# Squares of the query heads: turned by TensorE and summed by ScalarE, in place of two-column fp32 matmuls

## The chip, the cores and the metric

The kernel runs on one core of a Trainium2 chip. The metric is device time in microseconds of one execution. Four compute engines work side by side, each with its own instruction queue: TensorE (PE in the profile, its weight loads PEld), VectorE (DVE), ScalarE (ACT) and GpSimdE (POOL). SyncE (SP) issues most of the transfers. They wait for each other on semaphores only.

## The reference

Seven residual steps are computed on 512 tokens of width 1024: a feed-forward network, a mixer of three parts (windowed attention, a convolution, attention over a memory), another feed-forward network, and then two blocks of which the first has sparse attention and the second a short convolution as its mixer, each with a feed-forward network of its own. What matters here is the normalization of each head of 64 features of the queries, in both attention mixers:

```python
def rms_norm(x, g):
    y = xf * lax.rsqrt(jnp.mean(xf * xf, axis=-1, keepdims=True) + EPS)
    return (y * g).astype(x.dtype)
# first mixer
q = rope_partial(rms_norm(q.reshape(B, T, 8, 64), g_q), positions)
mq = rms_norm(mq.reshape(B, T, 4, 64), g_mq)
# second mixer
q = _rope(_rmsnorm(q.reshape(B, T, 16, 64), q_norm_g), positions)
```

For every token and every query head, the mean of 64 squares is needed, its root, and the inverse of that.

## The kernel before

Activations lie with features on the partitions and the 512 tokens along the free dimension. A weight tile of 1024 x 128 is split into a rounded high part and the rest, and a job multiplies it with the activations: for each of 8 chunks three matmuls with 512 columns (`product`, lines 705 to 713), 24 in all. ScalarE makes the high part (line 1223), VectorE (line 1587) or, inside the mixers, GpSimdE (line 619) the low part; SyncE loads tiles four jobs ahead.

Mixer A has 16 jobs (`TILES_A`: two convolution gates and values, kA, vA, the query tiles qA0 to qA3 and mq0, mq1, and the memory's keys and values mk0, mk1, mv0, mv1), mixer B has 18 (`TILES_B`: ki, wi, qi0 to qi3, vB0, vB1, kB0, kB1, qB0 to qB7). Each tile is 128 features, that is two heads. The order on every engine is written out by hand. In step m, TensorE does job m and, between its third and its fourth chunk (`betweenA`, `betweenB`, part 0), the small work for tile m - 1: `head_sum` (line 903), the spread of the inverse deviations of keys (`head_spread`, line 931), transposes of values (`turn_tile`). ScalarE, when a query tile's job is done, squares the tile into one half of `hsA` or `hsB` (`head_square`, line 1339), scales it (`head_scale`), makes a weight tile's high part (`lead`), and in mixer B turns index scores into `relu` (line 1551). It may only square into a half whose squares two tiles earlier have been read (`sq_read`).

Before the change, `head_sum` takes each block of 128 tokens of the squares as the stationary operand and multiplies with two columns of `mats`, ones for the first and for the second head. The result, tokens on the partitions and two columns per block, stays in bank 7 (mixer A) or bank 4 (mixer B) until all query tiles are done. Then `query_std` takes one root over the 48 or 64 columns, and VectorE's `query_inverse` (line 1861) takes the reciprocals and scales them; they are the scales of the exponentials in attention and of the maxima before them (`pair_max`, line 1871). Attention follows the last job directly: TensorE's first two pairs of scores, some matmuls on ones to pass the time (`idle`, line 731), and the third pair, which needs the first pair's exponentials.

VectorE has in mixer A the 62 taps of the convolution (line 1980, most of them in the steps of mixer A) and the ropes (lines 1855, 1857, 1859), and the memory's normalization (line 2018), in mixer B the sums of the index scores (line 2070), rounds of a top-128 selection (lines 2082 and 2084) and the ropes. A rope needs its tile with halves swapped, which SyncE does with four small DMAs (`swap_halves`, line 535). Keys use `head_sum`'s second half (line 926), which the change leaves alone, as it does the last query tile, qB7.

## Time and profile before

| | |
|---|---|
| median of 3 runs | 2119.54 us (2114.94 to 2120.14) |
| the profiled execution | 2114.27 us |
| its span, first to last instruction | 2112.1 us |
| TensorE busy | 2093.0 us, 99% |
| VectorE busy | 1242.8 us, 59% |
| ScalarE busy | 783.1 us, 37% |
| GpSimdE busy | 298.9 us, 14% |
| mean granted clock of TensorE | 0.999 |

In the rows below, times are in us from the start of the span unless marked ns. L917 is line 917 of the kernel. A timeline row has start, duration, engine, line, operation, output<-inputs, shape and count; behind it in brackets stands the engine's idle time before it and what ended that. Matmuls are pipelined, so the durations of neighbours overlap, and the distance of two starts is the time that one takes.

### The profile page before, as it was taken

What the parts mean: (1) busy time and instruction counts of PE and PEld (TensorE: products, weight loads), DVE (VectorE), ACT (ScalarE), POOL (GpSimd) and SP (SyncE); (2) the same over time, 40 slices, a digit from 0 to 9 for tenths busy, and PEclk for the clock granted to TensorE, in tenths of its full rate; (3) what the DMA queues carried; (4) which work ended last, traced back from release to release, by engine and by line L of the source; (5) the groups of instructions that cost most, each with busy time, mean ns of one, the idle gap of its engine ahead of it and who ended that gap; (6) DMA issues with size and microseconds to landing.
All of it is one profiled execution on the core that took longest, in us unless ns stands there. A gap on an engine that the chain in (4) does not pass through costs nothing.

```text
span 2112.1 us, 28230 instructions
## 1 busy us (share of the span) xinstructions
PE 2093.0 (99%) x9964; PEld 1718.3 (81%) x9968; DVE 1242.8 (59%) x1839; ACT 783.1 (37%) x1087; POOL 298.9 (14%) x357
## 2 busy tenths in 40 slices
PE   9999999999999999999999999999999999999999
PEld 7888888887888888877777888888888878888887
DVE  7666544786676654466995676654466456333332
ACT  6222333557442223334365442223343234222222
POOL 0122400650212230024300212210000000000000
PEclk9999999999999999999999999999999999999999
DMA  5556233320345542323300346542333222222232
GB/s 192 181 194 197 91 110 110 118 94 2 110 163 188 197 136 82 97 94 115 109 22 1 105 155 199 186 145 81 97 100 110 97 82 100 99 90 99 76 96 87
DMA packets 79572, 243.33 MB, mean 115 GB/s; under 512 B 12784, under 2 KB 13424, under 8 KB 79376
## 3 DMA queue, kind: packets, MB, share of 16 engines
q1 hardware_dynamic: 61376, 189.61, 27.5%
q0 software_dynamic: 18128, 52.84, 8.0%
q8 instruction: 40, 0.66, 0.1%
q14 instruction: 28, 0.23, 0.0%
HBM read 235.84 MB, written 2.29 MB: 113 GB/s over the span
## 4 chain that ended last, share of the span: by engine, by line
PE 92%; DVE 5%; ACT 1%; issue 1%; POOL 1%; DMA 0%; SPq 0%; ACTq 0%; DVEq 0%; POOLq 0%
PE ps L710 28%; PE ps L712 28%; PE ps L711 28%; PE ps L1014 2%; PE ps L972 1%; PE ps L993 1%; DVE ps L1980 1%; DVE tmp L1630 1%; DVE small L1876 1%; PE ps L975 0%; PE ps L1140 0%; POOL w_lo L619 0%; PE ps L917 0%; DVE qA L1859 0%; DVE ropA L1857 0%
## 5 line engine op out<-in xcount | busy, mean ns | idle before, releaser
L710 PE MATMUL ps<-h_hi,w_hi 128*128 128x512 f32 x1888 | 740.5, 392 | 2.8 <-issue 1.5
L712 PE MATMUL ps<-h_hi,w_lo 128*128 128x512 f32 x1888 | 735.4, 390 | 0.0
L711 PE MATMUL ps<-h_lo,w_hi 128*128 128x512 f32 x1888 | 735.2, 389 | 0.0
L1587 DVE TENSOR_TENSOR w_lo<-w_raw,w_hi 128x1024 fp32r<-128x1024 f32 x336 | 411.4, 1226 | 382.5 <-ACT w_hi L1223 368.0
L1223 ACT ACTIVATE w_hi<-w_raw 128x1024 fp32r<-128x1024 f32 x383 | 402.2, 1052 | 242.5 <-PE ps L712 240.7
L710 PEld LDWEIGHTS ps<-h_hi,w_hi 128*128 128x128 f32 x1888 | 353.8, 187 | 83.5 <-issue 8.8
L712 PEld LDWEIGHTS ps<-h_hi,w_lo 128*128 128x128 f32 x1888 | 353.7, 187 | 74.7
L711 PEld LDWEIGHTS ps<-h_lo,w_hi 128*128 128x128 f32 x1888 | 353.9, 187 | 73.1 <-issue 0.2
L710 PE MATMUL ps<-hid_hi,w_hi 128*128 128x512 f32 x704 | 274.1, 389 | 0.0
L711 PE MATMUL ps<-hid_lo,w_hi 128*128 128x512 f32 x704 | 274.0, 389 | 0.0
L712 PE MATMUL ps<-hid_hi,w_lo 128*128 128x512 f32 x704 | 274.0, 389 | 0.0
L619 POOL TENSOR_TENSOR w_lo<-w_raw,w_hi 128x512 fp32r<-128x512 f32 x100 | 132.7, 1347 | 531.4 <-ACT w_hi L1223 482.9
L1300 ACT ACTIVATE hid_hi<-tmp 128x512 f32 (+1 forms) x88 | 55.6, 632 | 393.6 <-DVE tmp L1763 384.8
L710 PEld LDWEIGHTS ps<-hid_hi,w_hi 128*128 128x128 f32 x704 | 132.2, 188 | 27.6
L711 PEld LDWEIGHTS ps<-hid_lo,w_hi 128*128 128x128 f32 x704 | 132.2, 188 | 27.3
L712 PEld LDWEIGHTS ps<-hid_hi,w_lo 128*128 128x128 f32 x704 | 132.2, 188 | 27.3
L1763 DVE TENSOR_TENSOR tmp<-tmp,ps 128x512 f32<-128x512 f32 x83 | 57.0, 687 | 132.3 <-PE ps L712 132.3
L1297 ACT ACTIVATE tmp<-ps 128x512 f32<-128x512 f32 x83 | 49.6, 598 | 223.4 <-PE ps L712 223.4
L1698 DVE SCALAR_TENSOR_TENSOR ada_sum<-ada_raw,c_act,ada_sum 128x512 f32<-128x512 f32 x168 | 125.9, 749 | 6.0 <-DMA ada_raw<-in_ada_w 1.8
L588 POOL DMA_DIRECT2D ada_raw<-in_ada_w x96 | 52.7, 549 | 393.5 <-DVE ada_sum L1698 372.8
L1704 DVE TENSOR_TENSOR hid_lo<-tmp,hid_hi 128x512 f32 (+1 forms) x88 | 61.4, 698 | 77.0 <-ACT hid_hi L1300 77.0
L1233 ACT ACTIVATE tmp<-x 128x512 f32 (+1 forms) x56 | 35.3, 631 | 158.1 <-DVE x L1609 157.7
(308 smaller groups left out, 1757.2 us busy)
## 6 DMA issues: line engine op xcount, KB each, us to landing
ada_raw<-in_ada_w POOLq DMA_DIRECT2D x96, 512.0 KB, 4.9
w_raw<-in_gate SPq DMA_DIRECT2D x88, 512.0 KB, 4.0
w_raw<-in_up SPq DMA_DIRECT2D x88, 512.0 KB, 3.5
w_raw<-in_down SPq DMA_DIRECT2D x64, 384.0 KB, 3.1
w_raw<-in_down SPq DMA_DIRECT2D x64, 320.0 KB, 2.8
w_raw<-in_w_mix_c SPq DMA_DIRECT2D x24, 512.0 KB, 3.4
w_raw<-in_w_mix_b SPq DMA_DIRECT2D x17, 512.0 KB, 3.5
w_raw<-in_w_mix SPq DMA_DIRECT2D x16, 512.0 KB, 3.5
```

What stands on the lines that cost most here:

```text
L588: pool.dma_start(ada_raw[:, (piece % 2) * 2 * ADA:(piece % 2 + 1) * 2 * ADA], src.rearrange("a p n -> (a p) n")).then_inc(ada_in[piece % 2 ...
L619: low = pool.tensor_tensor(w_lo[:, at:at + WT // 2], w_raw[:, at:at + WT // 2], f32(w_hi[:, at:at + WT // 2]), ALU.subtract)
L710: pe.matmul(dest, s_hi, m_hi, start=first and n == 0, stop=False)
L711: pe.matmul(dest, s_hi, m_lo, start=False, stop=False)
L712: mm = pe.matmul(dest, s_lo, m_hi, start=False, stop=last and n == len(pairs) - 1)
L1223: act.activation(chunk(w_hi, slot, WT), chunk(w_raw, slot, WT), ACT.Copy).then_inc(w_hi_done, 1)
L1297: act.activation(chunk(tmp, u), bank(s), ACT.Silu).then_inc(silu_done, 1)
L1300: act.activation(hid_hi[:, bass.ds(i * (2 * T) + u * T, T)], chunk(tmp, 2 + u), ACT.Copy)\
L1587: dve.tensor_tensor(chunk(w_lo, slot, WT), chunk(w_raw, slot, WT), f32(chunk(w_hi, slot, WT)), ALU.subtract).then_inc(w_lo_done, 1)
L1698: dve.scalar_tensor_tensor(ada_sum[:, :], w, c_act[:, k:k + 1], ada_sum[:, :], ALU.mult, ALU.add).then_inc(ada_sum_done, 1)
L1704: dve.tensor_tensor(hid_lo[:, at], chunk(tmp, 2 + u), f32(hid_hi[:, at]), ALU.subtract)\
L1763: dve.tensor_tensor(chunk(tmp, 2 + u), chunk(tmp, u), bank(s), ALU.mult)\
```

## The change

For 13 of the 14 query tiles (`TURNED_SQUARES`, all but qB7) `head_sum` transposes the four blocks of squares into the bank, tokens on the partitions and 128 features in a row. ScalarE's new `keep_squares` then reads each of the eight stretches of 64 columns (four blocks, two heads) with an ACTIVATE Identity whose `accum_out` is one column of `qstd`; the elementwise result goes back over the squares. It stands on ScalarE's queue behind the weight copy of the step and ahead of the index scores. The bank holds one tile at a time, so TensorE waits for `sq_kept` of the tile before, and ScalarE for the same two tiles on. `query_std` takes the root in place, and in mixer B a second one over qB7's eight columns; in mixer A it comes one step later on ScalarE (m == 14 in place of 13), and `query_inverse` one step later on VectorE (15 in place of 14).

```diff
--- before.py
+++ after.py
@@ -465,6 +465,13 @@
                        [("tabB", s) for s in ["pos"] + TAB])
         p_misc = Marks(sem("p_misc"), ["mem_total", "mem_spread", "conv_total", "conv_var", "conv_spread", "shift3", "ki_total", "shift4", "shift5", "shift6"])
 
+        TURNED_SQUARES = [t for t in SQUARES if is_query(t) and t != "qB7"]
+        sq_kept = Marks(sem("sq_kept"), TURNED_SQUARES)
+
+        def squares_of(t):
+            at = (h_sq.value[t] - 1) % 2 * T
+            return (hsA if t in TILES_A else hsB)[:, at:at + T]
+
         def query_column(pair):
             kind, j, b = pair
             return (j + 4 if kind == "mem" else j) * 2 * TT + b * 2
@@ -905,12 +912,20 @@
                 after(pe, h_sq, t)
                 n = h_sq.value[t] - 1
                 hs = hsA if mats is matsA else hsB
-                if is_query(t):
-
+                if t in TURNED_SQUARES:
                     if t == "qB0":
                         after(pe, h_std, "kB1")
-                    if t == "qA0":
+                    elif t == "qA0":
                         after(pe, a_misc, "mem_std")
+                    else:
+                        after(pe, sq_kept, TURNED_SQUARES[TURNED_SQUARES.index(t) - 1])
+                    for b in range(TT):
+                        mm = pe.transpose(bank(4 if t[1] == "B" else 7)[:, b * P:(b + 1) * P],
+                                          squares_of(t)[:, b * P:(b + 1) * P], mats[:, 0:P])
+                    mm.then_inc(sq_read.at(t), 1)
+                    return
+                if is_query(t):
+                    after(pe, sq_kept, "qB6")
                     q = QUERIES[t[1] == "B"].index(t)
                     for b in range(TT):
                         at = q * 2 * TT + b * 2
@@ -1340,8 +1355,19 @@
                 n = h_sq.value[t] - 1
                 W = M if t[:2] == "mk" else T
                 after_nth(act, sq_read, n - 2)
+                if n >= 2 and SQUARES[n - 2] in TURNED_SQUARES:
+                    after(act, sq_kept, SQUARES[n - 2])
                 act.activation(hs[:, (n % 2) * T:(n % 2) * T + W], tile_bank(t)[:, 0:W] if src is None else src,
                                ACT.Square).then_inc(h_sq.at(t), 1)
+
+            def keep_squares(t):
+
+                after(act, sq_read, t)
+                turned_, first = bank(4 if t[1] == "B" else 7), QUERIES[t[1] == "B"].index(t) * 2 * TT
+                for n in range(2 * TT):
+                    kept = act.activation(squares_of(t)[:, n * HD:(n + 1) * HD], turned_[:, n * HD:(n + 1) * HD], ACT.Identity,
+                                          accum_out=qstd[:, first + n:first + n + 1])
+                kept.then_inc(sq_kept.at(t), 1)
 
             def head_scale(t, gain, dest):
 
@@ -1368,9 +1394,15 @@
 
             def query_std(which, count):
 
-                after(act, sq_read, QUERIES[which == "B"][-1])
-                act.activation(qstd[:, 0:count], bank(4 if which == "B" else 7)[:, 0:count], ACT.Sqrt, bias=tiny[:, 0:1],
-                               scale=1.0 / HD).then_inc(a_misc.at("std" + which), 1)
+                turned = [t for t in QUERIES[which == "B"] if t in TURNED_SQUARES]
+                done = len(turned) * 2 * TT
+                after(act, sq_kept, turned[-1])
+                std = act.activation(qstd[:, 0:done], qstd[:, 0:done], ACT.Sqrt, bias=tiny[:, 0:1], scale=1.0 / HD)
+                if done < count:
+                    after(act, sq_read, QUERIES[which == "B"][-1])
+                    std = act.activation(qstd[:, done:count], bank(4)[:, done:count], ACT.Sqrt, bias=tiny[:, 0:1],
+                                         scale=1.0 / HD)
+                std.then_inc(a_misc.at("std" + which), 1)
 
             def head_std(t):
                 after(act, sq_read, t)
@@ -1467,6 +1499,8 @@
                     act.activation(sig[:, :], tile_bank(t), ACT.Sigmoid).then_inc(evac.at(t), 1)
                 if m < len(TILES_A):
                     lead(J + m)
+                if t in TURNED_SQUARES:
+                    keep_squares(t)
                 if t in h_std.value:
                     head_std(t)
                 if t == "vA":
@@ -1480,7 +1514,7 @@
                 if m == 9:
                     after(act, d_misc, ("mem", KC - 1))
                     act.activation(mh_hi[:, :], memx[:, :], ACT.Copy).then_inc(a_misc.at("mem_hi"), 1)
-                if m == 13:
+                if m == 14:
                     query_std("A", 8 * len(QUERIES[0]))
 
             def conv_part(u):
@@ -1541,6 +1575,8 @@
                     keep_tile(t, m - 1, values_place(vB, int(t[2]) * 2 * TT, 2 * TT))
                 if m == 4:
                     head_std("ki")
+                if t in TURNED_SQUARES:
+                    keep_squares(t)
                 if t in h_std.value:
                     head_std(t)
                 for b, h in index_step(m):
@@ -2020,7 +2056,7 @@
                 n = TILES_A[m - 2]
                 if n in h_normed.value:
                     head_norm(n, straight(n) if n == "kA" else chunk(mk, int(n[2]), M))
-                if m == 14:
+                if m == 15:
                     query_inverse("A", 8 * len(QUERIES[0]), qscA, qnsA)
 
             def conv_part(u):
```

## Rows read from the trace of the kernel before

**Rows 1.** Page, part 1: busy time, share of the span and count by engine.

```profile
PE 2093.0 (99%) x9964; PEld 1718.3 (81%) x9968; DVE 1242.8 (59%) x1839; ACT 783.1 (37%) x1087; POOL 298.9 (14%) x357
```

**Rows 2.** Page, part 4: the chain that ended last, shares by engine.

```profile
PE 92%; DVE 5%; ACT 1%; issue 1%; POOL 1%; DMA 0%; SPq 0%; ACTq 0%; DVEq 0%; POOLq 0%
```

**Rows 3.** Windows, engines busy in two stretches, one in each mixer: us, busy (count).

```profile
417.20:457.80 40.60, 39.74 (x231) 34.92 (x229) 39.68 (x51) 17.85 (x27) 26.84 (x19) 1.00 0.30 101
1009.50:1061.40 51.90, 51.21 (x267) 41.01 (x266) 49.63 (x102) 19.72 (x31) 18.65 (x14) 1.00 0.38 112
```

**Rows 4.** Timeline, TensorE, mixer A: the wait of the first memory key's spread.

```profile
457.87 0.66 PE L943 MATMUL ps<-identity,hrA 128*64 128x128 f32 x8 [0.94 <-DVE hrA L1836]
```

**Rows 5.** Timeline, VectorE, end of its chain in mixer A, and qA3's rope.

```profile
451.23 1.78 DVE L1857 TENSOR_TENSOR ropA<-pTA,ada_raw 128x512 f32<-128x512 f32 x1
...
457.65 0.17 DVE L1836 RECIPROCAL hrA<-hrA 128x4 f32<-128x4 f32 x1
```

**Rows 6.** Timeline, VectorE, end of mixer B and first pairs of attention B.

```profile
1060.74 0.69 DVE L1859 TENSOR_TENSOR qB<-ropB 128x512 f32<-128x512 f32 x1
1061.53 0.55 DVE L1863 RECIPROCAL qinv<-qstd 128x64 f32<-128x64 f32 x1
...
1066.03 0.42 DVE L1876 TENSOR_REDUCE small<-ps 128x2 f32<-128x256 f32 x1
```

**Rows 7.** Timeline, TensorE, sums for qB4: start us, us, engine, line, operation, count.

```profile
1042.04 0.39 PE L712 MATMUL ps<-h_hi,w_lo 128*128 128x512 f32 x1
...
1042.27 0.95 PE L917 MATMUL ps<-matsB,hsB 128*128 128x2 f32 x8
...
1043.39 0.39 PE L711 MATMUL ps<-h_lo,w_hi 128*128 128x512 f32 x1
```

**Rows 8.** Timeline, TensorE, four transposes of vB0.

```profile
978.42 0.60 PE L899 MATMUL ps<-identity,pB 128*128 128x128 f32 x4
978.95 0.70 PE L1140 MATMUL ps<-ki,qi 64*128 64x256 f32 x4
```

**Rows 9.** Timeline, ScalarE, mixer B: index scores, and the query tile qB4.

```profile
1015.30 1.09 ACT L1551 ACTIVATE relu<-ps 128x512 f32<-128x512 f32 x2 [2.98 <-PE ps L1140]
...
1040.42 0.60 ACT L1343 ACTIVATE hsB<-ps 128x512 f32<-128x512 f32 x1 [4.22 <-PE ps L712]
...
1041.49 1.06 ACT L1223 ACTIVATE w_hi<-w_raw 128x1024 fp32r<-128x1024 f32 x1
1046.76 0.60 ACT L1343 ACTIVATE hsB<-ps 128x512 f32<-128x512 f32 x1 [4.22 <-PE ps L712]
```

**Rows 10.** Source line 1364, the shortest ScalarE copy from PSUM: min/median/max ns, form.

```profile
L1364 ACT ACTIVATE wi<-ps x1: 177/177/177, 955.7 to 955.7; 128x32 f32<-128x32 f32 x1
```

**Rows 11.** Timeline, VectorE, mixer B: first index sum behind qB0.

```profile
1016.42 1.59 DVE L2070 SCALAR_TENSOR_TENSOR score<-relu,wi,score 128x512 f32<-128x512 f32 x2
```

**Rows 12.** Timeline, mixer A: memory halves, low weights, qA3's swap; last, kA's transfer (critical chain).

```profile
431.84 1.91 ACT L1482 ACTIVATE mh_hi<-memx 128x2048 fp32r<-128x2048 f32 x1
...
440.17 9.12 POOL L619 TENSOR_TENSOR w_lo<-w_raw,w_hi 128x512 fp32r<-128x512 f32 x6
...
443.18 2.64 SPq L552 DMA_DIRECT2D pTA<-qnA  x4
...
413.33 2.90 DMA pA<-pA
```

**Rows 13.** Windows, the granted clock (PEclk) at the start of attention B.

```profile
1061.00:1064.00 3.00, 2.85 (x21) 2.35 (x21) 2.76 (x9) 2.70 (x6) 0.00 (x0) 0.72 0.71 224
1064.00:1067.00 3.00, 3.00 (x22) 2.25 (x22) 2.28 (x6) 1.30 (x4) 0.00 (x0) 0.71 0.01 1
```

**Rows 14.** Timeline, TensorE, the idle matmuls of attention A and B, and the last sums.

```profile
467.45 1.13 PE L734 MATMUL ps<-ones 128*128 128x128 f32 x8
...
1060.09 1.05 PE L917 MATMUL ps<-matsB,hsB 128*128 128x2 f32 x8 [0.69 <-ACT hsB L1343]
...
1062.58 2.47 PE L734 MATMUL ps<-ones 128*128 128x128 f32 x10 [0.15 <-PE ps L975]
```

## Prediction, made before the change was run

> **What bounds the kernel now.** I read the page first, then the two stretches of the trace in which the edited lines run. TensorE is busy 99% of the span [rows 1] and 92% of the chain that ended last is its own [rows 2]. That invites the sum "time taken off TensorE comes off the kernel", and this change does take time off TensorE. But shares are averages over stages, and the edit touches only the two mixers, so the question is which engine ends each mixer.
>
> In [rows 3] stand two stretches, in mixer A from kA's rope to the wait at mk0, in mixer B from the job behind kB1 to the last rope before attention. In mixer A VectorE is busy 39.68 of 40.60 us, in mixer B 49.63 of 51.90 us, and it has 51 and 102 instructions there, so what is missing is the few hundredths between neighbours. TensorE looks as busy, 39.74 and 51.21, because it always has a tile to work on. Which of the two waits for the other at the end decides. In mixer A TensorE stands 0.94 us, until 457.87, for the reciprocal of mk0's deviation [rows 4], which VectorE reaches at 457.65 [rows 5], behind the convolution taps and the ropes in its queue. In mixer B VectorE ends the rope of qB6 at 1060.74 + 0.69 = 1061.43 and takes up the deviations 0.10 us later [rows 6]; without them no score of attention B gets its maximum. So VectorE paces mixer A, and in mixer B the two engines arrive together. None of VectorE's work is removed by the change.
>
> **What leaves and enters TensorE.** Thirteen query tiles (qA0 to qA3, mq0, mq1, qB0 to qB6) lose four fp32 matmuls with two columns, recorded as eight. Between the starts of the weight matmul before them and of the second one after them lie 1043.39 - 1042.04 = 1.35 us [rows 7]; without the sums these are two steps of 0.23, so a tile's sums cost 0.89 us, of which 0.09 falls on the first weight matmul behind them. Four transposes of the same size take 978.95 - 978.42 = 0.53 us from start to start [rows 8]; if the same 0.09 follows them, a tile saves 0.27 us, if not 0.36. I take 0.31: 13 x 0.31 = 4.0 us (3.5 to 4.7), 1.9 in mixer A and 2.2 in mixer B.
>
> On the transposes a rule speaks against the change. The row has them recorded at 0.60 us for four, and TensorE's granted clock is 1.00 over both stretches [rows 3, 8]. The Trainium skill ("TensorE: Matmul & The Clock Gate", Part 4: PE-mode transpose) says that transposes don't count as TensorE activity in the way that matmuls do, so that the full clock isn't reached on them. Here they would be half a microsecond in six, between fp32 weight matmuls; by the trace the sum stays as it is, by the rule the lower clock would come in, and that is the second rival below, worked out from rows.
>
> **Where the 4.0 us go.** In mixer A TensorE comes to mk0's spread 1.9 us earlier and waits 0.94 + 1.9 = 2.8 us there, still until 457.87. Behind that point its matmuls are the same as before, so mixer A gains 0. The moved steps (the root of the query sums one tile later on ScalarE, the reciprocals one tile later on VectorE) fall in VectorE's idle time before attention A and cost nothing as long as it has that idle time; if not, they cost under 1 us once. In mixer B the same: TensorE is 2.2 us early, VectorE still comes at 1061.43. Only the 0.10 us for which VectorE waited for the deviations are won.
>
> **What ScalarE gets.** For each of the 13 tiles eight ACTIVATEs of 64 columns from PSUM with a sum, put behind the weight copy. No row has one with a sum. The shortest copy from PSUM, 32 columns, took 0.177 us [rows 10], one of 512 took 0.60 [rows 9], so 64 columns take 0.177 + 32 x 0.42/480 = 0.205; neighbours overlap by about 0.10 (1040.42 + 0.60 against the next start, 1040.92) [rows 9]. Lower bound 0.105 each, 0.8 us a tile, if the sum costs nothing. Upper bound, no overlap and one more whole shortest instruction to hand over the sum: 0.38 each, 3.1 us a tile. I take 0.28, 2.2 us a tile: overlap was seen on every neighbour, but the sum has to leave the engine somehow. The Trainium skill ("ScalarE: Activation LUTs", What ACT_TABLE_LOAD costs) gives 186 ns + 0.833 ns per column and 93 ns of overlap; an estimate from that page is 0.146 each, 1.2 us a tile, within my bounds.
>
> The room for it: the weight copy of tile qB4 ends at 1042.55, the transposes at about 1042.27 + 0.60 = 1042.9, and the next tile's squares begin at 1046.76 [rows 7, 9], some 0.3 earlier now. So there are 3.6 us for the 2.2, and a late square hurts TensorE only after another 1.4 us, since the sums come nine weight matmuls (2.04 us) into the next job and a square takes 0.60. In most tiles the cost is nothing; the cover is ScalarE's 4.22 us of idle time per tile, and without it the price would be the 2.2 us each.
>
> Two places have less room. First, behind qB0 the index scores' ACTIVATEs queue behind the new ones. The transposes end at about 1013.8, the eight at 1016.0, the first score then at 1016.6; before it began at 1015.30 [rows 9], and VectorE wants it at 1016.42 [rows 11]. That is +0.2 us (0 to 1.1) on the engine that paces mixer B. Behind qB1 the same delay is already paid. Second, in mixer A the high half of the memory began at 431.84 right behind a weight copy [rows 12]; the eight ACTIVATEs of qA2 come in front of it, +2.2 us (0.8 to 3.1). GpSimdE's low half follows it, then its low weights, which began at 440.17, then SyncE's loads, and behind a load the four DMAs of qA3's swap, issued from 443.18 for 2.64 us. A transfer for kA landed 2.90 us after the last issue [rows 12]: 443.18 + 2.64 + 2.90 + 2.2 = 450.9, and VectorE uses it at 451.23 [rows 5]. So +0 (0 to 0.6). The weight jobs behind have more room than that.
>
> Sum against the profiled execution (2114.27 us, its span 2112.1): mixer A 0, mixer B +0.2 - 0.1, together +0.1. The median of the runs shown is 2119.54, 5.3 above the profiled one, and the runs scatter from 2114.94 to 2120.14; I add the sum to the median: 2119.6 us.
>
> **Rivals.** First, TensorE's lead isn't lost. For it: the page's shares, and in mixer B a near tie in which VectorE's lateness could partly come from waits that a faster TensorE shortens. Against it: VectorE's busy time in [rows 3]. It would give -4.0 (-4.7), and if the lowered clock at the start of attention B goes as well, 1.1 more: the ten idle matmuls before pair 2, which is reduced at 1066.03 [rows 6], would take 1.4 us in place of 2.47 [rows 14]. 2119.5 - 5.1 = 2114.4, at most 2113.7.
>
> Second, slower by the clock. TensorE stood 0.69 us for the squares of qB7 and then ran eight short matmuls [rows 14]; right behind, the granted clock is 0.72 and 0.71 in two windows of 3 us [rows 13], which is (0.28 + 0.29) x 3 / 0.5 = 3.4 us at 1.2 instead of 2.4 GHz. The idle matmuls show the price: 2.47 us for ten there, 1.13 us for eight in attention A [rows 14], 0.247 against 0.141 each; 3.4 us at the lower level lose 3.4 x (1 - 0.141/0.247) = 1.5 us of work. After the change TensorE stands 2.8 us at mk0's spread and about as long before attention B. If that lowers the clock in mixer A, where it was 1.00, behind the wait TensorE has only weight matmuls and is the last to finish: +1.5. If the lowered stretch of attention B moves from its idle matmuls onto its first pairs: +1.5 more. 2122.6 us; it decides from a wait somewhere above 0.94 us, which in mixer A left the clock at 1.00 [rows 3, 4].
>
> Third, slower by ScalarE: if an ACTIVATE with a sum takes much more than my upper bound. From 0.6 us each on (3.6 + 1.4 us of room over 8) TensorE waits at each tile's transposes. At 0.8 each the tile takes 6.4 + 2.1 + 0.35 = 8.9 us on ScalarE against 6.34 on TensorE (1046.76 - 1040.42): 13 x 2.5 = 33, less the wait in mixer A that swallows 0.94: 2151 us. Only an unseen stall between the two parts of the instruction speaks for it.
>
> Fourth, the change doesn't do what it says: transposes cost TensorE as much as the sums. Then nothing is early and the time is the same, 2119.7; only TensorE's rows tell it from my forecast.
>
> **How the numbers follow.** Forecast 0.62, TensorE's lead kept 0.13, clock 0.16, ScalarE 0.05, no saving 0.04. A difference of 0.3% is 6.4 us, about what a measurement of this kernel can tell from no change. Even the whole lead with the clock's 1.1 is 5.8, so faster gets 0.04, from both together with cheaper transposes. Slower gets the ScalarE case and a sliver of clock and late relu together, 0.06. The rest, 0.90, is within. The range: down to the whole lead, 2113.7, up to the clock case with the unknown costs at their upper ends, 2122.6 + 1.1 = 2123.7; it leaves out the ScalarE case and some of the runs' own scatter.
>
> **What the profile after would show.** If I am right, four transposes per query tile in place of eight two-column matmuls and the next weight matmul 0.5 to 0.6 us behind their start; at mk0's spread a wait of 2.5 to 3.2 us for VectorE's reciprocal; VectorE as dense as now in both mixers; before attention B a wait of TensorE for ScalarE's exponentials or VectorE of over 2 us; ScalarE's eight ACTIVATEs starting 0.15 to 0.35 us apart and its idle time before the squares shrunk to about 2 us. I would be wrong if VectorE's dense stretch ends earlier than before, relative to the start of its mixer, if TensorE waits for ScalarE at the transposes of most tiles, or if the granted clock is below 1.00 in mixer A.

## The result, and the profile after

The changed kernel takes 2123.14 us (median of 13 runs, 2119.63 to 2124.72). The kernel before, run beside it, takes 2115.13 us (13 runs, 2113.99 to 2120.14). The ratio is 1.0034, 95% interval [1.0026, 1.0042]: slower by 0.26 to 0.42%, about 7 us by the ratio and 8 us by the medians. The forecast was 2119.6 with a range of 2113.7 to 2123.7. The time lies in it by luck: forecast and range stood on a median of 2119.54 from three runs, which thirteen runs put at 2115.13. From that base the forecast is 2115.2 and the range ends at 2119.3, below what was measured. The forecast's own difference was +0.1 us. The measured one is that of no case but the second rival, in sign and place, and over twice its size (3.0 us).

The profile page's busy times and the chain that ended last (answering [rows 1, 2]):

```profile
PE 2098.6 (99%) x9912; PEld 1721.0 (81%) x9916; DVE 1245.1 (59%) x1839; ACT 805.3 (38%) x1296; POOL 298.6 (14%) x357
...
PE 89%; DVE 8%; issue 1%; ACT 1%; DMA 0%; SPq 0%; ACTq 0%; DVEq 0%
```

TensorE has 52 instructions fewer (13 x 4) and is busy 5.6 us longer: its matmuls have become slower, not more. VectorE's share of the chain rose from 5 to 8%. Now the windows, with the same columns as [rows 3, 13]: the granted clock is the figure behind POOL's busy time.

```profile
418.00:458.40 40.40, 35.71 (x201) 30.82 (x199) 39.52 (x48) 26.02 (x120) 28.80 (x20) 1.00 0.29 97
458.00:462.00 4.00, 3.52 (x21) 3.20 (x22) 1.02 (x4) 0.48 (x2) 1.05 (x1) 0.60 0.64 232
462.00:466.00 4.00, 4.00 (x25) 3.75 (x24) 0.00 (x0) 1.33 (x2) 0.90 (x1) 0.54 0.01 4
1013.10:1065.00 51.90, 51.06 (x254) 39.52 (x253) 49.76 (x103) 33.69 (x146) 18.64 (x14) 0.98 0.38 111
1064.00:1067.00 3.00, 2.10 (x10) 1.80 (x9) 2.83 (x10) 0.52 (x2) 0.00 (x0) 0.50 0.85 258
1067.00:1070.00 3.00, 2.57 (x15) 1.82 (x16) 2.40 (x5) 1.37 (x4) 0.00 (x0) 0.50 0.02 4
1080.00:1083.00 3.00, 3.00 (x14) 1.96 (x14) 1.68 (x5) 1.33 (x4) 0.00 (x0) 0.50 0.02 5
```

VectorE is as dense in both mixers as before (39.52 of 40.40, 49.76 of 51.90), so it does pace them. TensorE lost 4.0 us of busy time in mixer A's stretch (39.74 to 35.71): that is its waiting. Behind mixer A the granted clock is at its lower level, 1.2 GHz, from 458.8 to 465.6, 6.8 us; at the start of attention B from 1063.0 to 1083.5, 20.5 us, where the kernel before had 3.4 us and went back to the upper level at 1065.7, in its third pair, which followed the idle matmuls without a wait. A third stretch of 3.4 us begins at 1711.5. TensorE's timeline at the two places, with the transposes of one tile between (answering [rows 4, 7, 14]):

```profile
458.48 0.83 PE L958 MATMUL ps<-identity,hrA 128*64 128x128 f32 x8 [4.77 <-DVE hrA L1872]
...
469.22 0.49 PE L987 MATMUL ps<-kA,qA 64*128 64x128 f32 x4
...
1044.26 0.39 PE L719 MATMUL ps<-h_hi,w_lo 128*128 128x512 f32 x1
1044.49 0.60 PE L923 MATMUL ps<-matsB,hsB 128*128 128x128 f32 x4
1044.85 0.47 PE L717 MATMUL ps<-h_hi,w_hi 128*128 128x512 f32 x1
1045.16 0.39 PE L718 MATMUL ps<-h_lo,w_hi 128*128 128x512 f32 x1
...
1061.02 1.05 PE L932 MATMUL ps<-matsB,hsB 128*128 128x2 f32 x8 [0.69 <-ACT hsB L1360]
...
1063.63 2.47 PE L741 MATMUL ps<-ones 128*128 128x128 f32 x10
1067.43 0.80 PE L987 MATMUL ps<-kB,qB 64*128 64x128 f32 x4 [1.33 <-ACT pB L1421]
...
1082.10 0.61 PE L990 MATMUL ps<-dmask,ident16B 128*128 128x256 bf16 x2
```

The same places in the kernel before, attention A's first score and attention B's third pair and first score with `dmask`:

```profile
465.64 0.49 PE L972 MATMUL ps<-kA,qA 64*128 64x128 f32 x4
...
1064.98 0.80 PE L972 MATMUL ps<-kB,qB 64*128 64x128 f32 x4
...
1074.16 0.39 PE L975 MATMUL ps<-dmask,ident16B 128*128 128x256 bf16 x2
```

From the weight matmul ahead of the transposes to the second behind them it is 1045.16 - 1044.26 = 0.90 us, before 1.35 [rows 7]: a tile saves 0.45, and the distance of two tiles agrees (6.34 to 5.91, 0.43). The saving is there. At mk0's spread it becomes a wait of 4.77 us.

From the traces of both kernels the loss adds up. In mixer A the spread begins at 458.48, before at 457.87: +0.61. From there to attention A's first score it is 10.74 us, before 465.64 - 457.87 = 7.77: +2.97, at the lower clock. Together +3.6. Until attention B's third pair (1067.43 against 1064.98) TensorE regains 1.1. From there to the first score with `dmask` it is 1082.10 - 1067.43 = 14.67 us, before 9.18: +5.5. At the end of attention B the offset is 8.1, behind the stretch at 1711.5 it is 9.6, and 2121.7 - 2112.1 = 9.6 are the spans. The last 1.5 us aren't shown to be the change's: the wait ahead of that stretch is 2.34 us here and 2.37 in the kernel before, and before_no_idle and before_apart, which have nothing of the change, have the same stretch. The profiled run is one of the longer ones (2123.87).

ScalarE, one tile in mixer B (answering [rows 9]):

```profile
1043.71 1.06 ACT L1238 ACTIVATE w_hi<-w_raw 128x1024 fp32r<-128x1024 f32 x1
1045.13 0.22 ACT L1368 ACTIVATE hsB<-ps 128x64 f32<-128x64 f32 x1 [0.35 <-PE ps L923]
1045.25 0.20 ACT L1368 ACTIVATION_READ_ACCUMULATOR hsB<-ps 128x1 f32 x1
1045.34 0.22 ACT L1368 ACTIVATE hsB<-ps 128x64 f32<-128x64 f32 x1
1045.44 0.20 ACT L1368 ACTIVATION_READ_ACCUMULATOR hsB<-ps 128x1 f32 x1
...
1048.55 0.60 ACT L1360 ACTIVATE hsB<-ps 128x512 f32<-128x512 f32 x1 [1.68 <-PE ps L719]
```

A sum is two instructions, and the next pair starts 0.20 us later (1045.13, 1045.34, 1045.54): 1.6 us a tile. Then ScalarE still waits 1.68 us for TensorE. VectorE in mixer A, with GpSimdE beside it, and at the end of mixer B (answering [rows 5, 6]):

```profile
414.69 1.77 DVE L1893 TENSOR_TENSOR ropA<-pA,ada_raw 128x512 f32<-128x512 f32 x1
...
424.68 1.79 DVE L1893 TENSOR_TENSOR ropA<-pTA,ada_raw 128x512 f32<-128x512 f32 x1
426.51 1.66 DVE L1895 TENSOR_TENSOR qA<-ropA 128x512 f32<-128x512 f32 x1
...
458.25 0.17 DVE L1872 RECIPROCAL hrA<-hrA 128x4 f32<-128x4 f32 x1
...
1064.30 0.69 DVE L1895 TENSOR_TENSOR qB<-ropB 128x512 f32<-128x512 f32 x1
1064.91 0.55 DVE L1899 RECIPROCAL qinv<-qstd 128x64 f32<-128x64 f32 x1
```

```profile
424.62 3.00 POOL L626 TENSOR_TENSOR w_lo<-w_raw,w_hi 128x512 fp32r<-128x512 f32 x2 [3.85 <-ACT w_hi L1238]
```

The same two in the kernel before:

```profile
425.30 0.69 DVE L1857 TENSOR_TENSOR ropA<-pTA,ada_raw 128x512 f32<-128x512 f32 x1
...
425.68 3.15 POOL L619 TENSOR_TENSOR w_lo<-w_raw,w_hi 128x512 fp32r<-128x512 f32 x2 [4.29 <-ACT w_hi L1223]
```

VectorE's work in mixer A starts 0.62 to 0.64 us earlier than before, yet the reciprocal comes 0.60 later: VectorE is 1.24 us slower there. 1.1 of it is one instruction, the second rope operation of qA0: 1.79 us here, 0.69 before, when GpSimdE's low weights began behind it and not ahead of it. GpSimdE had waited for ScalarE's weight copy, which began at 424.54 before and at 423.48 now. The hand-over at the end of mixer B did shrink: the reciprocal began 0.10 us behind the last rope before and begins 0.08 ahead of its end now (1064.91 against 1064.99), so 0.2 us are won.

### The profile page after: what moved, and what is told of

Read it like the earlier page. It is cut to its first block, busy times and chain, and to the rows that moved or that the text cites. A ratio compares the mean times of both kernels' runs of the same rounds, so it can differ in the third digit from the quotient of the medians.

```text
span 2121.7 us, 28346 instructions
## 1 busy us (share of the span) xinstructions
PE 2098.6 (99%) x9912; PEld 1721.0 (81%) x9916; DVE 1245.1 (59%) x1839; ACT 805.3 (38%) x1296; POOL 298.6 (14%) x357
## 4 chain that ended last, share of the span: by engine, by line
PE 89%; DVE 8%; issue 1%; ACT 1%; DMA 0%; SPq 0%; ACTq 0%; DVEq 0%
PE ps L717 28%; PE ps L719 27%; PE ps L718 27%; PE ps L1029 2%; DVE ps L2016 1%; PE ps L987 1%; PE ps L1008 1%; DVE score L2120 1%; DVE top L2118 1%; DVE tmp L1666 1%; PE ps L990 1%; DVE small L1912 0%; DVE ropA L1893 0%; PE ps L1155 0%; DVE qA L1895 0%
```

## The experiments

Three theories. **Clock**: TensorE's saved time turns into waits, the clock falls behind them, and what follows runs at half speed. **ScalarE**: the sums or their late arrival cost the time. **Work**: the longer mixers themselves, or the moved steps, cost it. Medians in us; the last column lists the stretches at the lower clock in the profiled run, as start (length) in us, without the one at the very end.

| kernel | time (runs) | before beside it | ratio [95%] | at 1.2 GHz |
|---|---|---|---|---|
| copy_sums | 2121.43 (8) | 2115.06 | 1.0026 [1.0014, 1.0038] | 455.6 (6.8), 1066.6 (13.7), 1708.3 (3.4) |
| a_only | 2118.15 (12) | 2115.06 | 1.0015 [1.0003, 1.0027] | 456.6 (10.2), 1067.6 (3.4), 1159.7 (10.2), 1712.7 (3.4) |
| b_only | 2118.34 (12) | 2115.06 | 1.0011 [1.0003, 1.0020] | 1064.1 (13.7), 1705.8 (3.4) |
| fill_ab | 2116.14 (12) | 2115.06 | 1.0004 [0.9995, 1.0014] | 460.4 (3.4), 1156.8 (10.2), 1709.7 (3.4) |
| before_no_idle | 2119.03 (11) | 2114.87 | 1.0012 [1.0003, 1.0022] | 1063.8 (13.7), 1705.5 (3.4) |
| fill_b | 2121.89 (9) | 2114.87 | 1.0031 [1.0021, 1.0042] | 458.3 (6.8), 1062.5 (3.4), 1158.1 (10.2), 1711.0 (3.4) |
| fill_long | 2118.99 (11) | 2114.87 | 1.0009 [0.9998, 1.0021] | 1155.8 (10.2) |
| b_only_fill_long | 2117.67 (11) | 2114.87 | 1.0002 [0.9992, 1.0013] | 1067.9 (10.2), 1706.2 (3.4) |
| before_all_filled | 2115.55 (11) | 2115.05 | 1.0000 [0.9991, 1.0009] | none |
| after_all_filled | 2117.23 (11) | 2115.05 | 1.0008 [0.9999, 1.0017] | 1061.5 (3.4) |
| before_apart | 2113.63 (11) | 2115.09 | 0.9996 [0.9986, 1.0007] | 1061.5 (3.4), 1153.6 (3.4), 1703.2 (3.4) |
| after_filled_apart | 2114.70 (12) | 2115.09 | 1.0000 [0.9991, 1.0009] | none |

The ratio compares means. The kernel before has some late runs (near 2119.5) in each set, which raise its mean and not its median, so the ratio shows less than the two medians do. The last column is one run of each kernel, and not a typical one everywhere: the profiled run took 2124.79 in a_only, 2121.82 in fill_ab and 2123.06 in fill_b, above the medians.

**copy_sums**: ScalarE without its sums; one copy of eight columns stands in their place.

```diff
-                for n in range(2 * TT):
-                    kept = act.activation(squares_of(t)[:, n * HD:(n + 1) * HD], turned_[:, n * HD:(n + 1) * HD], ACT.Identity,
-                                          accum_out=qstd[:, first + n:first + n + 1])
+                kept = act.activation(qstd[:, first:first + 2 * TT], turned_[:, 0:2 * TT], ACT.Copy)
```

> Part of the computation is left out: of each turned tile ScalarE copies eight columns in place of summing eight stretches of 64. TensorE's instructions are those of the changed kernel. Theory C (the clock: TensorE comes early to a wait, stands longer, and the granted clock falls to its lower level for 6.8 us in mixer A and 20.5 us in attention B): the time stays near the changed kernel's, 5 to 8 us above the kernel before, with a wait of 4 to 5 us at mk0's spread and both low stretches there. Theory S (the 104 pairs of ACTIVATE and accumulator read, 1.57 us a tile on ScalarE, delay what follows them): the loss goes, within 1.5 us of the kernel before.

2121.43, near the changed kernel's 2123.14; the intervals of the ratios overlap. TensorE waits again at mk0's spread, and the clock falls behind both waits:

```profile
456.76 1.12 PE L958 MATMUL ps<-identity,hrA 128*64 128x128 f32 x8 [3.26 <-DVE hrA L1870]
```

Three quarters or more of the loss are there without the sums (6.4 of 8.0 us by the medians). ScalarE's sums aren't the cause of the bulk of it. The wait is 1.5 us shorter than the changed kernel's: here qA0's second rope operation took 0.68 us, not 1.79, by a near tie with GpSimdE (started 0.04 us behind it, in the changed kernel 0.06).

**a_only** and **b_only**: only one mixer's query tiles turned, the other's as before with its waits and steps in their old places. The main line of a_only's edit (b_only has TILES_B):

```diff
-        TURNED_SQUARES = [t for t in SQUARES if is_query(t) and t != "qB7"]
+        TURNED_SQUARES = [t for t in SQUARES if is_query(t) and t != "qB7" and t in TILES_A]
```

> Only mixer A's six query tiles are turned. Theory C: mixer A loses what it lost in the changed kernel, about 3 us by the clock and 1.2 us because VectorE comes 1.2 us later to mk0's reciprocal (ropes 1.1 us longer beside GpSimdE's low weights); attention B has the short low stretch of the kernel before, 3.4 us. In all 3 to 4.5 us above the kernel before. Theory S: six thirteenths of the loss, 3.3 us, but without a low clock in mixer A.

> Only mixer B's seven query tiles are turned. Theory C: no low clock in mixer A and its wait at mk0's spread 0.9 us as before; at the start of attention B the idle matmuls end before the first exponentials are there, TensorE waits 1 to 1.5 us and the clock stays low for 15 to 20 us: 3 to 5 us above the kernel before. Theory S: the index scores behind qB0 and qB1 come late, at most 1 us, and no low stretch longer than before.

+3.1 and +3.3 us, together 6.4 of the whole 7 to 8, and each has its long low stretch in its own place, a_only in mixer A and b_only at the start of attention B: a_only waits 4.77 us at mk0's spread, b_only 0.94 as before.

```profile
456.00:466.00 10.00, 7.29 (x36) 6.77 (x36) 3.14 (x7) 1.82 (x4) 3.52 (x4) 0.53 0.32 107
```

```profile
456.00:466.00 10.00, 8.72 (x75) 7.26 (x75) 3.65 (x10) 4.20 (x8) 5.08 (x5) 1.00 0.41 145
```

These are the windows behind mk0's spread, a_only first, b_only second: clock 0.53 and 1.00. These are two losses of one kind. a_only's profiled run has 10.2 us more at the lower clock at 1159.7, so it shows where the clock fell in mixer A, and not what its median run looks like.

**fill_ab**: the changed kernel, its waits filled with matmuls on ones that nobody reads.

```diff
             def head_spread(t):
+                if t == "mk0":
+                    after(pe, sq_kept, "mq1")
+                    idle(14)
                 after(pe, h_rstd, t)
...
+            after(pe, i_relu, IDX[-1])
+            idle(2)
             betweenB(len(TILES_B), 0)
...
-            attention(PAIRS_B, scoreB, lambda pair: pair_turn(pair, pB, T, matsB), valuesB, sumsB, "stdB", 5)
+            attention(PAIRS_B, scoreB, lambda pair: pair_turn(pair, pB, T, matsB), valuesB, sumsB, "stdB", 12)
```

> The changed kernel with matmuls on ones in the waits: 14 at mk0's spread, 2 ahead of qB7's sums, 12 in place of 5 before attention B's third pair. Theory C: granted clock 1.00 in mixer A and in attention B, mixer A loses only VectorE's 1.2 us, attention B starts its third pair 1 us earlier than in the kernel before: -1.5 to +1 us against the kernel before. Theory S: the fill changes nothing, 6 to 8 us above it.

2116.14: more work for TensorE and 7.0 us less time than the changed kernel. It is 1.1 us above the kernel before, at the upper edge of what was expected, and in mixer A a wait of 1.64 us and a low stretch of 3.4 us are left, where clock 1.00 was expected. Three of the twelve runs, those at a mean granted clock of 1.00, took 2113.8 to 2114.4. The rows of its start of attention B:

```profile
1061.72 2.92 PE L741 MATMUL ps<-ones 128*128 128x128 f32 x24
1065.66 0.49 PE L990 MATMUL ps<-kB,qB 64*128 64x128 f32 x4 [1.03 <-ACT pB L1426]
```

**before_no_idle**: the kernel before, none of the change in it.

```diff
-            attention(PAIRS_B, scoreB, lambda pair: pair_turn(pair, pB, T, matsB), valuesB, sumsB, "stdB", 5)
+            attention(PAIRS_B, scoreB, lambda pair: pair_turn(pair, pB, T, matsB), valuesB, sumsB, "stdB", 0)
```

> The kernel before, with none of its idle matmuls between the first two score pairs of attention B and the third (5 in each of two places before); nothing of the change is in it. If the clock theory holds (a stretch in which TensorE waits ahead of attention B lets the granted clock fall, and the sparse score pairs that follow at half speed don't raise it again), this kernel loses by the same mechanism as the changed one: a low stretch of 10 to 20 us beginning near 1063 in place of 3.41, and a median 3 to 5 us above before. If the rival holds (the longer low stretch comes from the turned squares or ScalarE's load in mixer B), there is none here: the low stretch stays at 3.41 us and the time stays within 1 us of before.

+4.2 us by the medians, 1.0012 by the ratio, for leaving five matmuls out. (They stand in one place and not in two; the trace records each as two.) The third pair now waits 1.63 us. The clock:

```profile
1061.00:1071.00 10.00, 8.16 (x50) 6.64 (x48) 6.12 (x19) 6.49 (x18) 0.00 (x0) 0.64 0.13 36
1071.00:1081.00 10.00, 10.00 (x61) 7.23 (x60) 6.62 (x19) 4.72 (x13) 0.00 (x0) 0.68 0.01 2
```

The long low stretch of attention B needs no turned square. This is the theory's strongest support: a loss of the same kind, made without the change.

**fill_b**: fill_ab without its part in mixer A.

> The changed kernel with idle matmuls at mixer B's end alone (2 ahead of qB7's sums, 12 in place of 5 between the first pairs of attention B); mixer A's wait of 4.8 us is left as it is. The clock theory: mixer B's share comes back (b_only lost 3.3 us, the changed kernel 7 to 8), so the time is 2117.5 to 2119.5, near that of a_only (2118.2), with a low stretch of 3.4 to 10 us at mixer A's spread and none of over 3.5 us near 1063. The rival (time lost to work itself that comes later in mixer B): 2122 to 2124 as the changed kernel, whatever the clock shows.

A miss. The start of attention B was repaired as expected (3.4 us low instead of 20.5), but the time is 2121.9. In the profiled run 10.2 us at the lower clock lie at the end of attention B instead:

```profile
1154.00:1168.00 14.00, 12.83 (x70) 12.34 (x69) 3.10 (x7) 1.71 (x3) 0.00 (x0) 0.65 0.00 1
```

There TensorE stands 1.17 us for ScalarE in the kernel before as in the changed one, and the clock sometimes falls behind it and sometimes not. By its time alone fill_b sides with the rival; against that stands fill_ab, which differs only by mixer A's fill and lies 1.1 us above the kernel before. That fill is worth 5.8 us here, more than the 3.1 that a_only lost; the rest stays unexplained.

**fill_long** (21 and 16 idle matmuls in place of 14 and 12) and **b_only_fill_long** (b_only, with 2 and 16).

> Both fills, longer: 21 idle matmuls at mk0's spread in place of 14, 16 in place of 12 between the first pairs of attention B. With 14 a wait of 1.64 us and a low stretch of 3.41 us were left in mixer A. The clock theory: both go, 2114 to 2116, and most runs at a mean granted clock of 0.998 or more; 0.43 us a tile saved on TensorE stays worth nothing, because VectorE sets the pace, so it isn't faster than before by 0.3%. A rival, that the fills were hiding a loss of another kind and longer ones cost time: 2117 or more.

> Only mixer B's tiles turned, and mixer B's end filled as in fill_long (2 and 16). Mixer A is as before. The clock theory: 2113.5 to 2115.5, the same as before within 0.1%, and the low stretch near 1063 gone or 3.41 us. If turning the squares in mixer B cost time by itself (ScalarE's 1.6 us a tile), the 3.3 us of b_only stay in part: 2117 or more.

In fill_long both places are clean at last, no wait at mk0's spread and clock 1.00 up to 1155.8, in the last pairs of attention B:

```profile
453.69 4.85 PE L741 MATMUL ps<-ones 128*128 128x128 f32 x42
458.63 0.66 PE L961 MATMUL ps<-identity,hrA 128*64 128x128 f32 x8
...
456.00:466.00 10.00, 9.46 (x84) 8.59 (x83) 5.34 (x11) 2.59 (x6) 5.61 (x5) 1.00 0.31 108
```

Yet its runs fall apart: five at 2115.2 to 2116.1, six at 2119.0 to 2121.0, and the profiled run, one of the six, has 10.2 low us at 1155.8. b_only_fill_long is a miss of the same kind: two runs at 2113.9 and 2114.0, the others at 2116.5 to 2118.7, the profiled one with 10.2 low us at 1067.9, behind a wait of 1.51 us. Both medians are over the 2117 of the rival, so the times alone don't refute it. In the two profiled runs there are low stretches left to carry the loss.

The traces separate the clock from the work. From mk0's spread to attention A's first score it takes 7.74 to 7.77 us in every kernel without a low stretch there, changed (fill_long, after_all_filled, after_filled_apart) or not; with 3.4 us at the lower clock it takes 9.25 (fill_ab), with 6.8 it takes 10.25 to 10.74 (copy_sums, fill_b, the changed kernel), with 10.2 it takes 11.35 (a_only). So the moved steps cost nothing, and the 2.97 us are the clock's. At the start of attention B the third pair waited 1.03 us in fill_ab and the pairs went on at the upper level; behind waits of 1.63 (before_no_idle) and 2.58 us (b_only, copy_sums) 13.7 us at the lower level followed.

**before_all_filled** and **after_all_filled**: the waits behind which a low stretch had been seen are filled, in the kernel before and in the changed one. The two edits that fill_ab doesn't have:

```diff
+                if pair == PAIRS_B[-1]:
+                    idle(10, 0)
                 if X >= 1:
                     kept_before(PAIRS[X - 1])
...
+            idle(18)
             project("outC", 6, y_lo_done, KC + 2, yC_hi, yC_lo)
```

> The kernel before with every wait of TensorE behind which a profile has shown a low stretch filled by idle matmuls: 2 at mixer B's end, 10 in place of 5 between the first pairs of attention B, 10 ahead of the last pair's turn (the wait of 1.17 us near 1154), 18 ahead of mixer C's output (the wait of 2.37 us near 1700). The clock theory: no low stretch but the one at the very end, a median of 2112.5 to 2114.5, and none of the runs at 2118 to 2121 that before has in about a third. A rival, that those late runs have another cause than these waits: the same two groups of times as before.

> The changed kernel with the same waits filled, and mk0's spread too (21), with 16 between the first pairs of attention B. It is the change at full clock: the difference from before_all_filled is what turned squares are worth by themselves. The theory of the prediction (VectorE paces both mixers, so 0.43 us a tile saved on TensorE buys nothing but waits): 0 to 1.5 us above before_all_filled, 2113 to 2115.5. The rival, that the saving would show once the clock is held up: 2 us or more below before_all_filled, 2109 to 2112.

before_all_filled: nine runs within 2115.2 to 2116.0 at clock 1.00, the last two 2117.3 and 2117.4; the late group that the kernel before has (2118 to 2120 in 6 of 21 runs beside it) is gone. It is no faster, though, so the expected 2112.5 to 2114.5 was missed by a microsecond: idle matmuls that end late cost what the clock gave. At the last pair TensorE starts 1.00 us behind the end of ScalarE's copy (1154.11 to 1155.11), 0.06 in the kernel before; at mixer C's output 1.66 us behind the end of VectorE's `y_lo` (1701.95 to 1703.61), 0.27 before. Together that is 2.3 us. after_all_filled: 2117.23, 1.7 us above, a little over the expected 1.5, with overlapping intervals of the ratios. So at nearly full clock the change still buys nothing, and by these medians it costs 1 to 2 us more. Three of its eleven runs lie at 2120.1 to 2120.8: here the late group isn't gone. Attention A's first score comes at 466.60, in before_all_filled at 464.75: the difference lies in mixer A, whose wait, all filled now, is still 4.85 us long. The prediction had 2.8.

**before_apart** and **after_filled_apart**: VectorE and GpSimdE kept apart at qA0. after_filled_apart has 12 idle matmuls at mk0's spread in place of 21.

```diff
             for j in range(LEAD, len(TILES_A) + KC):
+                if j == 11:
+                    after(pool, h_roped, "qA0")
                 split(first_job["mixA"] + j)
```

> The kernel before with one wait more: GpSimdE takes the low weights of job 11 of mixer A only once qA0's rope is done. Two of VectorE's rope operations of one form took 0.69 us in one place and 1.66 to 1.79 in another, and the long ones lie beside GpSimdE's low weights. If the collision is real, qA0's last rope operation takes 0.69 in place of 1.65 us, VectorE comes to mk0's reciprocal about 1 us earlier against the mixer's start, TensorE's wait of 0.94 us there goes, and the time is 2113.5 to 2115, up to 1 us below before. If the long durations belong to the operation itself (its operands, or something else), nothing moves: 1.65, 0.94 and 2115.

> after_all_filled with the same wait of GpSimdE, and 12 idle matmuls in place of 21 at mk0's spread. There qA0's second rope operation took 1.79 us and its last 1.67. By the collision theory both take 0.69, VectorE paces mixer A 2 us faster, mk0's spread comes 2 us earlier, and the time is 2 us lower: 2114.5 to 2116 against 2117.2, at or just above before; TensorE's wait at mk0's spread, the filled part with it, shrinks from 4.85 to 2.8 us, which is the prediction's figure. If the collision isn't the cause of mixer A's larger wait: 2.0 us of wait open behind the 12 idle matmuls, and 2117 or more.

VectorE and GpSimdE in after_filled_apart:

```profile
424.38 0.68 DVE L1903 TENSOR_TENSOR ropA<-pTA,ada_raw 128x512 f32<-128x512 f32 x1
425.10 0.69 DVE L1905 TENSOR_TENSOR qA<-ropA 128x512 f32<-128x512 f32 x1
...
425.87 2.54 POOL L626 TENSOR_TENSOR w_lo<-w_raw,w_hi 128x512 fp32r<-128x512 f32 x2 [5.41 <-DVE qA L1905]
...
433.26 0.69 DVE L1903 TENSOR_TENSOR ropA<-pTA,ada_raw 128x512 f32<-128x512 f32 x1
...
434.13 5.45 POOL L689 TENSOR_TENSOR mh_lo<-memx,mh_hi 128x512 fp32r<-128x512 f32 x4 [5.71 <-ACT mh_hi L1526]
...
453.25 2.84 PE L743 MATMUL ps<-ones 128*128 128x128 f32 x24
454.30 0.17 DVE L1882 RECIPROCAL hrA<-hrA 128x4 f32<-128x4 f32 x1
456.02 0.66 PE L963 MATMUL ps<-identity,hrA 128*64 128x128 f32 x8
```

qA0's two rope operations take 0.68 and 0.69 us in place of 1.79 and 1.67, and GpSimdE's two 2.54 in place of 3.0. What wasn't expected: VectorE now comes to qA1's ropes (433.26) before GpSimdE's low half of the memory begins (434.13), so that collision goes too; one at qA2 is added (1.71 us for its first rope operation, which took 0.68 in the changed kernel). The reciprocal is ready from 454.47 on, 1.2 us behind TensorE's arrival at 453.25; the real wait is 1.2 us, and the fill was 1.5 us too long. The spread comes at 456.02, not 458.86, and the time is 2114.70, 2.5 us below after_all_filled, of which the shorter fill may be a part. Its runs, too, fall apart, seven at 2113.9 to 2114.8 and five at 2117.7 to 2118.2 with a lower mean clock (0.997 to 0.998 against 0.999 to 1.000), though the waits are filled. In before_apart TensorE's wait of 0.94 us at mk0's spread is gone and the median is 2113.63 against 2115.09; the ratio, 0.9996 [0.9986, 1.0007], can't tell it from no change. Neither version beats the kernel before by more than can be measured.

## Why the prediction was right or wrong

**What bounds the mixers: right.** VectorE stayed dense and its lateness set the end. Of TensorE's saving 1.1 us reached attention B's third pair, for a reason that the first rival names: before, the idle matmuls at the lower clock ended 0.9 us after TensorE could have gone on (its third pair starts 0.95 us behind ScalarE's first exponentials now, 1066.48 to 1067.43, and 1.88 before, 1063.10 to 1064.98). The rest was spent waiting. That after_all_filled isn't faster than before_all_filled shows it nearly without the clock.

**The saving on TensorE: too small.** 0.43 a tile, not 0.31. The term for four transposes, 0.53 from start to start, came from [rows 8]; in their place among weight matmuls it is 1044.85 - 1044.49 = 0.36. A larger saving meant a longer wait: 6 x 0.43 = 2.6 us in mixer A, not 1.9.

**"mixer A gains 0", still until 457.87: wrong.** The step treated VectorE's schedule as fixed while TensorE got faster. But TensorE's jobs release ScalarE's weight copies and these GpSimdE's low weights; they moved forward with it, and GpSimdE's fell on qA0's rope: +1.1 us on the pacing engine. after_filled_apart takes the collisions at qA0 and qA1 away, and the wait shrinks to 1.2 us. The wait is then 0.94 + 2.6 + 1.2 = 4.8, as measured. The rows that show the price were there in part: 1.78 for a rope operation of the form that elsewhere takes 0.69 [rows 5, 6]. What lay beside it, GpSimdE's low weights from 451.05 on, wasn't among them.

**ScalarE: right.** 1.6 us a tile inside bounds of 0.8 and 3.1 (2.2 taken), cover left over (1.68 us). The +0.2 us at the first index sum behind qB0 didn't come: VectorE starts it at 1020.24, which is 1016.42 plus the 3.82 us that lie between the two kernels there. An estimate from the Trainium skill ("ScalarE: Activation LUTs", What ACT_TABLE_LOAD costs) was 1.2 us a tile; the trace has 0.10 to 0.12 from an ACTIVATE to its read, less than the 0.146 of that estimate, and 0.09 to 0.10 more for the read, which it leaves out. The memory's high half began at 432.39, 0.55 us later than before (431.84) and 1.2 against the mixer's start, where 2.2 was taken. The third rival has nothing for it.

**Mixer B: right** until the clock, to 0.3 us. The two kernels lie 3.82 us apart on VectorE behind qB0 and 3.56 at the end of the last rope (1064.99 against 1061.43).

**The second rival, given 0.16, is what happened.** This is the step that failed: the sum priced TensorE's longer waits at nothing, "mixer A gains 0" and mixer B +0.1, and the runs showed the lower clock behind them, +3.0 us in mixer A and +5.5 in attention B. The rival's price for a microsecond at the lower level held in mixer A: 1.5 lost in 3.4, 0.44, against 2.97 / 6.83 = 0.43. In attention B it is 0.34 (5.5 us in the 16.1 from 1067.43 to 1083.5). What failed in the rival is the length. It took 3.4 us for each stretch, the only length in the trace before, and that one had lain mostly over idle matmuls. With a wait of 1.33 us behind the idle matmuls and then the attention's first pairs it is 20.5 us, and they run at half speed to 1083.5. The forecast had the wait of 2.8 us before it and the fall behind 0.69 us and eight short matmuls [rows 14]; to hold the forecast at 0.62 against that was the mistake of weight. At mk0's spread an open wait of 3.3 to 4.8 us had the lower clock beside it in all four kernels with one, 1.64 us in fill_ab too (3.4 us of it), and 0.94 in none of the five with that; before the runs only the last was known.

**The rule on transposes.** The low clock came, but not on transposes: with them in every query tile the granted clock is 1.00 over mixer A's stretch above, and in after_filled_apart over the whole span but its last 0.5 us. The Trainium skill ("TensorE: Matmul & The Clock Gate", Part 4: PE-mode transpose) says that transposes don't count as activity as matmuls do. No run here shows it: half a microsecond of them in six left the clock where it was.

**The base.** 4.4 us of the forecast's 2119.6 are the scatter of three runs. Of the kernel before's runs most lie near 2114.9 and a sixth to a third near 2119.5. None of its late runs was profiled; their mean clock is 0.995 to 0.998, that of the others 0.997 to 0.999. In the profiled runs of fill_ab (2121.8) and fill_long (2119.0), which lie among the late ones of their kernels, 10 us at the lower clock lie at the end of attention B.

**Open.** Why the same wait of 1.17 us near 1154 is followed by the lower clock in some executions and not in others, and why fill_b seems to meet it in every run. before_all_filled, where that wait is filled, has no late group, which fits the clock but doesn't explain the choice; after_all_filled and after_filled_apart, where it is filled as well, have one, and no late run of theirs was profiled. At the end of mixer B, too, seven kernels have a wait of only 0.24 us ahead of qB7's sums; fill_b and after_all_filled have a low stretch of 3.4 us there, 1.4 and 2.2 us behind the sums, the other five none. Whether the remaining 1.1 us between after_filled_apart and before_apart are the change or its idle matmuls (1.5 us too long at mk0's spread, 0.9 at attention B's last pair, 1.4 at mixer C's output) wasn't separated.

## What to carry to other kernels

Time taken off an engine that isn't the last to arrive becomes a wait, and for TensorE a wait has a price of its own: read the granted clock behind each wait and ask how dense the work there is, because it decided here whether 3 or 20 us ran at half speed. Filling the wait with matmuls gave the loss back but won nothing: no filled kernel is measurably faster than the kernel before, and a fill that outlasts the wait costs its excess. And when an engine gets faster, move everything that it releases forward too, and look what that lands beside; a collision on the pacing engine cost the full amount here (1.1 us).

## What the runs showed of the hardware

The same sparse work ran at either level of the clock. In fill_long attention B's first pairs ran at 1.00 throughout; behind a wait TensorE was down over the same pairs for 13.7 us in b_only and before_no_idle and 20.5 in the changed kernel.

A VectorE TENSOR_TENSOR on 128x512 with both inputs in SBUF takes 0.69 us alone and up to 1.79 (mostly 1.66 to 1.79) when it starts while a TENSOR_TENSOR of GpSimdE is running. Where VectorE's starts first, as at 443.42 in the changed kernel, 0.06 us ahead, it keeps 0.68 and GpSimdE's takes 1.77 in place of 1.3; in copy_sums it kept 0.68 even when it started 0.04 us behind. The convolution taps, with one input in PSUM, take 0.78 in both cases (five in 3.91 us at 447.43, beside GpSimdE). The Trainium skill ("GPSIMD Engine Reference", 1. Specifications) names contention with VectorE instructions that have two SBUF inputs; the trace agrees, and before_apart and after_filled_apart show it by taking it away.

A ScalarE sum along the free dimension is two instructions, ACTIVATE and ACTIVATION_READ_ACCUMULATOR, and a pair over 64 columns from PSUM goes by every 0.20 us.
